# Two-layer decoder on one core: weight buffers cut into 1 MiB slots, the second round of an expert set moved, one loop over the set pairs

## The chip, the cores and the metric

The kernel runs on one core of a Trainium2 chip. The metric is the device time of one execution in microseconds; lower is better. One stretch of the clock of TensorE matters below: the profile shows which share of full speed (2.4 GHz) was granted, 1.0 or 0.5 (1.2 GHz).

## The reference, cut to what matters

Two layers over 256 tokens of width 1024, all float32. Each layer is attention and then a mixture of 32 experts.

```python
x = x + concat[DiffAttn(h), StickBreaking(h)] @ w_out[l]        # h = rms_norm(x) @ w_in[l], 3072 columns
h2 = rms_norm(x)
# routing: the best group of 4, then the best 2 of its 8 experts
hg = einsum('sd,edf->sef', h2, w_gate)      # w_gate, w_up: (32, 1024, 256)
hu = einsum('sd,edf->sef', h2, w_up)
act = silu(hg) * hu * combine[..., None]    # combine is zero but for 2 experts of a token
x = x + einsum('sef,efd->sd', act, w_down)  # w_down: (32, 256, 1024)
```

All 32 experts' weights are read in each layer: 3 MiB an expert, 96 MiB a layer, beside 16 MiB of `w_in` and `w_out`.

## The kernel before, in words

Every engine has its own program, and semaphores tie them together. SyncE (`SP`) issues the weight DMAs in one order written by hand; TensorE (`PE`) multiplies; VectorE (`DVE`) and ScalarE (`ACT`) copy PSUM banks out and do the pointwise work.

Attention of a layer: `proj_tile` multiplies the normed tokens with six blocks of `w_in` (2 MiB each, 512 columns), the heads' scores and sums follow, and `out_proj` uses two blocks of `w_out`.

Experts of a layer: they are done in 8 sets of 4 (`LANES`). Of each expert up to 32 tokens (`SLOTS`) are taken in a round, so that 4 experts fill the 128 rows. One set is, in TensorE's order in `expert_set`: `gate_up` (64 matmul records, two for each float32 matmul, from gate and up weights of 4 experts), `gather` of the tokens of the following set (32 records), `transpose_weights` for it, `transpose_act`, `down` (32 records), `scatter` back to the tokens (8 records). If an expert of the set has more than 32 tokens, a second round is done by the branches on `most > SLOTS`: before, `early` (its gather, its transpose of the weights, its `gate_up`) stands between the first round's `transpose_act` and its `down`, and `late` (its `down` and `scatter`) at the set's end. Rounds three and up are in `further_rounds`; when there is no second round TensorE branches over `late` and `whole`, and increments seven or eight semaphores (L333) in their place.

TensorE's sets stand in a loop over pairs of sets (a set with even number and one with odd number use other slots of the weight buffer). Before, it is two loops: three passes over the pair's code, and a second copy of that code for the last pair, which reads the last `w_down` elsewhere. VectorE and ScalarE have one loop each.

Weight buffers before: `wbuf` has slots of 2 MiB and `dnbuf` holds the four `w_down` of a set. SyncE's `load_rest` waits for `slot_used` (the set before has done its `gate_up` in all its rounds), issues one gate, then the next set's lane 0, then waits for `dn_used`, issues the four `w_down` and the rest of the next set's gate and up.

VectorE in a set: `select` for the following set (and for the second round), `activate`, `act_copy` (which lets `down` start), `gather_copy`, `y_copy`, `into_x`.

## Time and profile before

| what | value |
|---|---|
| time, median of 3 runs | 855.61 us (848.56, 855.61, 856.1) |
| span of the profiled execution | 850.2 us, first to last instruction |
| granted TensorE clock, mean of the span | 0.940 |
| busy: PE, DVE, ACT | 687.0, 310.9, 123.8 us |
| read from HBM | 238.54 MB, 282 GB/s over the span |
| experts of layer 0 / of layer 1 | about 175.7 to 424 us / 594.5 to 845 us |

The profiled execution's time from start to end of the device's work isn't listed apart from its span; the median of the runs is 5.4 us above the span. A line number such as L1159 is the line of the kernel before; `PEldq` is TensorE's instruction sequencer; "issue" is time of an engine for which the profile shows no awaited work. Profiles number the microseconds from the first instruction.

### The profile page before, as it was taken

The page shows a single profiled execution, that of the slowest core. Times are in us where ns is not written, and L with a number is a line of the kernel's source. Part 1 is how long each engine was busy: PE and PEld are TensorE (multiplying, and loading weights), DVE is VectorE, ACT ScalarE, POOL GpSimd, SP SyncE. Part 2 cuts the span into 40 slices and gives each one's busy share as a digit, 9 for nine tenths or more (in the row PEclk, how much of TensorE's full clock was granted, in tenths as well). Part 3 has the DMA queues.
Part 4 walks back from the last instruction along what each step waited for, and adds up shares of the span by engine and source line. Part 5 has one row for each costly group of instructions (what it writes and reads, how often), then busy time and mean ns, then how long its engine had stood idle before and what let it go on. Part 6 is the DMA issues. An engine that isn't in the chain of part 4 may idle for free.

```text
span 850.2 us, 10581 instructions
## 1 busy us (share of the span) xinstructions
PE 687.0 (81%) x3752; PEld 341.8 (40%) x3753; DVE 310.9 (37%) x692; ACT 123.8 (15%) x302; POOL 9.0 (1%) x19
## 2 busy tenths in 40 slices
PE   7998999887487487787799989997874874777885
PEld 4445464553133133252344445647331331332423
DVE  0437622543223223333325363425332331333333
ACT  3115421200000000000031343211000000000100
POOL 0000000010000000000020000000000000000000
PEclk9998999999889799899999999998987997998999
DMA  8894046759999999957297220492599999999441
GB/s 288 275 391 161 1 180 269 292 116 383 417 419 402 419 398 420 420 228 310 90 356 285 100 99 24 182 422 115 190 423 417 373 422 418 387 422 420 183 167 52
DMA packets 49815, 240.93 MB, mean 283 GB/s; under 512 B 7424, under 2 KB 7712, under 8 KB 25152
## 3 DMA queue, kind: packets, MB, share of 16 engines
q1 hardware_dynamic: 49120, 238.61, 70.4%
q0 software_dynamic: 608, 0.99, 1.0%
q8 instruction: 74, 1.21, 0.6%
q14 instruction: 13, 0.11, 0.0%
HBM read 238.54 MB, written 1.05 MB: 282 GB/s over the span
## 4 chain that ended last, share of the span: by engine, by line
PE 66%; issue 17%; PEldq 5%; DVE 4%; ACT 2%; PEld 2%; DVEq 1%; DMA 1%; ACTq 1%; SPq 0%
PE bank L1014 18%; PE bank L1159 17%; PE bank L1140 9%; PE bank L1185 7%; PE bank L1112 6%; PEldq L1178 4%; PE bank L1071 1%; ACT qkT L533 1%; PE bank L1058 1%; PEld bank L1176 1%; PE bank L1176 1%; DMA wbuf<-in_w_in 1%; PE bank L1091 1%; PE bank L1034 1%; PEldq L1323 1%
## 5 line engine op out<-in xcount | busy, mean ns | idle before, releaser
L1159 PE MATMUL bank<-wbuf,qkT 128*32 128x512 f32 x1024 | 137.7, 686 | 80.8 <-issue 79.6
L1014 PE MATMUL bank<-wbuf,hTbuf 128*128 128x512 f32 x384 | 170.1, 600 | 2.5 <-DMA wbuf<-in_w_in 2.0
L1159 PEld LDWEIGHTS bank<-wbuf,qkT 128*32 128x32 f32 x1024 | 39.1, 124 | 176.9 <-issue 175.3
L1014 PEld LDWEIGHTS bank<-wbuf,hTbuf 128*128 128x128 f32 x384 | 72.5, 192 | 90.8 <-issue 88.5
L1140 PE MATMUL bank<-qkT,xn 128*128 128x128 f32 x576 | 70.1, 281 | 20.2 <-issue 20.2
L1140 PEld LDWEIGHTS bank<-qkT,xn 128*128 128x128 f32 x576 | 67.0, 195 | 34.7 <-issue 34.6
L787 DVE TENSOR_TENSOR x_sb<-x_sb,bank 128x512 f32<-128x512 f32 x72 | 46.2, 684 | 77.2 <-PE bank L1185 77.2
L1176 PE MATMUL bank<-dnbuf,qkT 128*32 128x512 f32 x512 | 61.6, 597 | 11.4 <-DVE qkT L776 7.7
L764 DVE TENSOR_SCALAR qkT<-qkT 128x256 f32<-128x256 f32 x18 | 5.3, 294 | 156.4 <-ACT qkT L529 156.4
L1112 PE MATMUL bank<-wbuf,hTbuf 128*128 128x512 f32 x128 | 56.0, 593 | 0.0
L529 ACT ACTIVATE qkT<-bank 128x256 f32<-128x256 f32 x18 | 6.9, 384 | 287.5 <-PEq L1162 287.5
L1185 PE MATMUL bank<-qkT,hTbuf 128*128 128x512 f32 x80 | 36.7, 601 | 8.4 <-ACT qkT L533 8.4
L1112 PEld LDWEIGHTS bank<-wbuf,hTbuf 128*128 128x128 f32 x128 | 23.9, 190 | 27.7 <-issue 27.7
L1176 PEld LDWEIGHTS bank<-dnbuf,qkT 128*32 128x32 f32 x512 | 15.1, 109 | 49.5 <-issue 49.3
L1185 PE MATMUL bank<-qkT 128*128 128x512 f32 x64 | 29.3, 600 | 5.4 <-ACT qkT L533 5.4
L766 DVE RECIPROCAL qkT<-qkT 128x256 f32<-128x256 f32 x18 | 31.5, 1752 | 1.4
L474 ACT ACTIVATE wbuf<-bank,rstd 128x512 f32<-128x512 f32 x24 | 16.4, 684 | 78.8 <-PE bank L1014 78.5
L1185 PEld LDWEIGHTS bank<-qkT,hTbuf 128*128 128x128 f32 x80 | 14.4, 189 | 31.5 <-issue 31.5
L525 ACT COPY qkT<-bank 128x512 f32<-128x512 f32 x18 | 10.6, 586 | 90.0 <-PE bank L1140 90.0
L533 ACT COPY qkT<-bank 128x512 f32<-128x512 f32 x18 | 10.6, 586 | 87.8 <-PEq L1178 87.8
L1185 PEld LDWEIGHTS bank<-qkT 128*128 128x128 f32 x64 | 11.5, 190 | 22.1 <-issue 22.1
L780 DVE COPY qkT<-bank 128x512 f32<-128x512 f32 x18 | 12.4, 690 | 18.7 <-PEq L1178 18.7
(187 smaller groups left out, 580.9 us busy)
## 6 DMA issues: line engine op xcount, KB each, us to landing
wbuf<-in_w_gate SPq DMA_DIRECT2D x64, 1024.0 KB, 12.5
wbuf<-in_w_up SPq DMA_DIRECT2D x64, 1024.0 KB, 16.8
dnbuf<-in_w_down SPq DMA_DIRECT2D x56, 1024.0 KB, 10.7
wbuf<-in_w_in SPq DMA_DIRECT2D x10, 2048.0 KB, 18.4
wbuf<-in_w_out SPq DMA_DIRECT2D x4, 2048.0 KB, 18.0
wbuf<-in_w_down SPq DMA_DIRECT2D x8, 1024.0 KB, 12.2
wbuf<-in_w_in SPq DMA_DIRECT2D x4, 1024.0 KB, 8.5
x_sb<-in_x SPq DMA_DIRECT2D x2, 512.0 KB, 4.1
```

Source lines behind the costliest of these rows:

```text
L474: nc.scalar.activation(dst, ps[PROJ_BANK[i][t]][:, :], ACT.Copy, scale=rstd[:, t:t + 1]).then_inc(proj_out, 1)
L533: nc.scalar.copy(y[:, HALF:], ps[5][:, :]).then_inc(s["y_a"], 1)
L766: V.reciprocal(rg, rg)
L780: V.tensor_copy(y[:, 0:HALF], ps[4][:, :]).then_inc(s["y_d"], 1)
L787: last = V.tensor_tensor(x_sb[:, t, c], x_sb[:, t, c], ps[SC_BANK[t][h]][:, :], ALU.add)
L1014: last = MM(ps[PROJ_BANK[i][t]][:, :], hT[:, k, t * P:(t + 1) * P], w[:, k, :], start=(k == 0), stop=(k == KC - 1))
L1112: last = MM(ps[OP_BANK[t][h]][:, :], hT[:, k, t * P:(t + 1) * P], w[:, k, :], start=(k == 0), stop=(k == KC - 1))
L1140: last = MM(ps[k // 4][:, (k % 4) * P:(k % 4 + 1) * P], xn[:, t, k * P:(k + 1) * P], sel[:, t, :], start=(t == 0), stop=(t == TT - 1))
L1159: MM(ps[2][j * SLOTS:(j + 1) * SLOTS, :].rearrange("p (a f) -> p a f", a=2), src[:, k, j * SLOTS:(j + 1) * SLOTS], halves[:, gate:up + 1:u ...
L1176: MM(ps[4 + h][j * SLOTS:(j + 1) * SLOTS, :], actT[:, c, j * SLOTS:(j + 1) * SLOTS], at[j][:, c * D + h * HALF:c * D + (h + 1) * HALF], st ...
L1178: pe.drain().then_inc(s[f"dn{h}_ps"], 1)
L1185: last = MM(ps[SC_BANK[t][h]][:, :], weights[:, t, :], y[:, h * HALF:(h + 1) * HALF], start=True, stop=True)
```

## The change

- One buffer of 19 slots of 1 MiB holds all weights and the attention's scratch. Which slot holds what is a table with a period of two sets (`GATE_SLOT`, `UP_SLOT`, `DOWN_SLOT`, `BLOCK_SLOT`). The total stays 19 MiB.
- SyncE's program is written out set by set, without its loop. It waits for the products themselves (`proj_ps`, `qkT_ps`, `o_ps`, `oproj_ps`) in the attention, and for `gu_used` and `dn_used`, one count for each set, among the experts. After the last set it loads three blocks of the next layer's `w_in` at once, and the rest behind the last `gate_up` and `down`.
- TensorE has one loop over four pairs instead of three passes and a copy.
- The second round: its gather and weight transposes stand at the set's start, its `gate_up` right behind that of the first round (in PSUM bank 3), its `transpose_act` and `down` after the first round's `scatter` has been added in.
- VectorE does `gather_copy` before `act_copy`, no longer behind it. Reading `most` moves from behind `gate_up` to the set's start.

```diff
-        wbuf = sb("wbuf", [P, (SLOTS_W + 1) * SLOT + SLOT // 2])
-        dnbuf = sb("dnbuf", [P, LANES, FC * D])
+        wbuf = sb("wbuf", [P, SLOTS_W * SLOT])
...
+            def load_further_sets(l):
+                for g in range(1, SETS):
+                    if g > 1:
+                        for j in range(LANES - 1):
+                            load_up(l, g, j)
+                    sp_.wait_ge(gu_used, l * SETS + g)
+                    load_up(l, g, LANES - 1)
+                    if g + 1 < SETS:
+                        for j in range(LANES):
+                            load_gate(l, g + 1, j)
+                    sp_.wait_ge(dn_used, l * SETS + g)
                     for j in range(LANES):
+                        load_down(l, g, j)
+            def load_next_layer(l):
+                for i in range(3):
+                    load_block(l, i)
+                sp_.wait_ge(gu_used, l * SETS)
+                load_block(l, 3)
+                load_block(l, 4)
+                sp_.wait_ge(dn_used, l * SETS)
+                load_block(l, 5)
+                load_half(l, IN_BLOCKS, 0)
...
             def expert_set(l, g, parity):
                 most = dve.value_load(cnt[0:1, bass.ds(g, 1)], min_val=0, max_val=SEQ)
...
+                with dve.If(most > SLOTS):
+                    select(more, g, 1, sel_more, selw_more)
+                    gather_copy(more, dve.snap(g * MORE + (l * SETS * MORE + 1)), hgT_more, selwT_more, more_half)
                 dve.wait_ge(first["selwT_ps"], g + (l * GATHERS + 1))
                 select(first, g + 1, None, sel, selw)
-                with dve.If(most > SLOTS):
-                    select(more, g, 1, sel_more, selw_more)
                 n = dve.snap(g + l * SETS + 1)
-                activate(first, n)
-                act_copy(first, n)
-                gather_copy(first, dve.snap(g + l * GATHERS + 2), hgT, selwT2[1 - parity], 6)
+                activate(first, n, FIRST_GU)
+                gather_copy(first, dve.snap(g + l * GATHERS + 2), hgT, selwT2[1 - parity], first_half)
+                act_copy(first, n, first_half)
+                with dve.If(most > SLOTS):
+                    activate(more, dve.snap(g * MORE + (l * SETS * MORE + 1)), MORE_GU)
                 y_copy(first, n)
...
-            def expert_set(l, g, parity, last):
-                for j in range(LANES):
-                    pe.wait_ge(gu_in[parity][j], g * 16 + (l * SETS + 2 - parity) * 16)
-                gate_up(first, g + (l * GATHERS + 1), hgT, l, parity)
+            def expert_set(l, pair, parity):
+                g = pe.snap(pair * 2 + parity)
                 most = pe.value_load(cnt[0:1, bass.ds(g, 1)], min_val=0, max_val=SEQ)
                 n = pe.snap(g + l * SETS + 1)
...
+                with pe.If(most > SLOTS):
+                    m = pe.snap(g * MORE + (l * SETS * MORE + 1))
+                    pe.wait_ge(first["hg_d"], g + (l * GATHERS + 1))
+                    pe.wait_ge(first["hg_a"], g + (l * GATHERS + 1))
+                    pe.wait_ge(x_moe, n)
                     pe.wait_ge(x_more, m)
                     gather(more, m, sel_more)
+                    transpose_weights(more, m, more_half, selw_more)
+                arrived = pe.snap(pair * 16 + (l * SETS // 2 + 1) * 16)
+                for j in range(LANES):
+                    pe.wait_ge(gate_in[parity][j], arrived)
+                    pe.wait_ge(up_in[parity][j], arrived)
+                gate_up(first, pe.snap(g + (l * GATHERS + 1)), FIRST_GU, hgT, parity)
+                with pe.If(most > SLOTS):
+                    m = pe.snap(g * MORE + (l * SETS * MORE + 1))
+                    gate_up(more, m, MORE_GU, hgT_more, parity)
                     pe.wait_ge(more["selwT_out"], m)
+                with pe.If(most <= 2 * SLOTS):
+                    pe.sem_inc(gu_used, 1)
+                following = pe.snap(g + (l * GATHERS + 2))
+                gather(first, following)
...
+                def late(m):
+                    pe.wait_ge(x_moe, g + (l * SETS + 2))
+                    transpose_act(more, m, more_half)
+                    down(more, m)
...
-                with pe.Fori(0, SETS // 2 - 1) as pair:
-                    expert_set(l, pe.snap(pair * 2), 0, False)
-                    expert_set(l, pe.snap(pair * 2 + 1), 1, False)
-                with pe.Fori(SETS // 2 - 1, SETS // 2) as pair:
-                    expert_set(l, pe.snap(pair * 2), 0, False)
-                    expert_set(l, pe.snap(pair * 2 + 1), 1, True)
+                with pe.Fori(0, SETS // 2) as pair:
+                    for parity in range(2):
+                        expert_set(l, pair, parity)
```

## Rows read from the trace of the kernel before

**Rows 1.** The page: busy time of the engines, the chain's shares by engine

```profile
PE 687.0 (81%) x3752; PEld 341.8 (40%) x3753; DVE 310.9 (37%) x692; ACT 123.8 (15%) x302; POOL 9.0 (1%) x19
...
PE 66%; issue 17%; PEldq 5%; DVE 4%; ACT 2%; PEld 2%; DVEq 1%; DMA 1%; ACTq 1%; SPq 0%
```

**Rows 2.** Chain of waits in order of time: start us, us, what

```profile
223.40 10.84 issue
234.23 9.80 PE bank L1159 x64
...
259.13 2.11 issue
261.24 2.77 PE bank L1159 x21
264.01 1.02 issue
265.03 5.34 PE bank L1159 x43
270.37 1.26 issue
...
346.71 4.56 issue
351.27 9.31 PE bank L1159 x64
...
644.61 11.05 issue
...
679.37 3.61 issue
682.98 8.77 PE bank L1159 x64
691.75 1.28 issue
693.03 3.83 PE bank L1140 x32
...
768.57 4.99 issue
```

**Rows 3.** The gate weights that set 4 needs last: their issue, then landing

```profile
L360 SPq DMA_DIRECT2D wbuf<-in_w_gate x1: 333/333/333, 271.5 to 271.5; - x1
...
DMA to landing us min/median/max: 13.0/13.0/13.0
```

**Rows 4.** Waits of SyncE's queue: us in total, times, longest us

```profile
SPq L360 <- PEq L1195: 203.3, 12, 27.8
```

**Rows 5.** Chain of waits between 637 and 732 us, one loop-back step by step

```profile
705.53 3.34 issue
708.87 0.07 PEldq L331
...
710.47 6.05 PEldq L1323
```

**Rows 6.** Branches and reads of TensorE's sequencer: ns min/median/max, first and last start

```profile
L1323 PEldq COMPARE_BRANCH  x6: 76/6009/6189, 227.6 to 772.9; - x6
...
L1245 PEldq COMPARE_BRANCH  x16: 68/226/362, 193.8 to 839.0; - x16
...
L1190 PEldq EVENT_SEMAPHORE  x22: 51/51/51, 173.6 to 820.9; - x22
```

**Rows 7.** DMA queue of the instructions: packets, MB, share

```profile
q8 instruction: 74, 1.21, 0.6%
```

**Rows 8.** TensorE's timeline through set 6 (layer 0), with second round

```profile
367.09 3.84 PE L1140 MATMUL bank<-hTbuf,xn 128*128 128x128 f32 x32 [1.11 <-DVE qkT L758]
370.76 0.38 PE L1147 MATMUL bank<-cst,hTbuf 128*128 128x128 f32 x2
371.71 7.07 PE L1159 MATMUL bank<-wbuf,hTbuf 128*32 128x512 f32 x64 [0.56 <-DVE hTbuf L758]
...
387.82 3.96 PE L1176 MATMUL bank<-dnbuf,qkT 128*32 128x512 f32 x32
392.59 3.67 PE L1185 MATMUL bank<-qkT,hTbuf 128*128 128x512 f32 x8 [0.81 <-ACT qkT L533]
```

**Rows 9.** VectorE's timeline between 365 and 368 us

```profile
366.01 0.42 DVE L776 COPY qkT<-bank 128x256 f32<-128x256 f32 x1 [1.61 <-PE bank L1167]
366.35 0.68 DVE L758 COPY qkT<-bank 128x512 f32<-128x512 f32 x1
366.95 0.41 DVE L760 COPY hTbuf<-bank 128x256 f32<-128x256 f32 x1
```

**Rows 10.** Busy time by stretches of 10 us (PE, PEld, DVE, ACT, POOL; clock, DMA share, GB/s)

```profile
350.00:360.00 10.00, 8.73 (x64) 2.55 (x64) 3.16 (x17) 0.00 (x0) 0.00 (x0) 0.71 1.01 419
...
370.00:380.00 10.00, 8.79 (x83) 3.21 (x85) 1.66 (x4) 0.97 (x2) 0.00 (x0) 1.00 0.11 43
```

More of the change, by code:

```diff
@@ L302, in decoder @@
         GATHERS = SETS + 1
-        def second_round_early(eng, n_set, most, early):
-            with eng.If(most > SLOTS):
-                early(eng.snap(n_set * MORE + 1))
         def further_rounds(eng, n_set, most, late, whole, owed):
@@ L533, in y_copy, with whole, expert_set @@
                 nc.scalar.copy(y[:, HALF:], ps[5][:, :]).then_inc(s["y_a"], 1)
-            def early(n):
-                gather_copy(more, n, hgT_more)
-                gate(more, n)
-            def late(n):
-                y_copy(more, n)
-            def whole(n, r):
-                early(n)
-                late(n)
+            def whole(m, r):
+                gather_copy(more, m, hgT_more)
+                gate(more, m, MORE_GU)
+                y_copy(more, m)
+            def expert_set(l, g):
+                most = act.value_load(cnt[0:1, bass.ds(g, 1)], min_val=0, max_val=SEQ)
+                n = act.snap(g + l * SETS + 1)
+                with act.If(most > SLOTS):
+                    gather_copy(more, act.snap(g * MORE + (l * SETS * MORE + 1)), hgT_more)
+                gate(first, n, FIRST_GU)
+                with act.If(most > SLOTS):
+                    act.wait_ge(first["act_out"], n)
+                    gate(more, act.snap(g * MORE + (l * SETS * MORE + 1)), MORE_GU)
+                gather_copy(first, act.snap(g + l * GATHERS + 2), hgT)
+                y_copy(first, n)
+                further_rounds(act, g + l * SETS, most, lambda m: y_copy(more, m), whole, ACT_MORE)
             for l in range(DEPTH):
@@ L609, in _ @@
                 with act.Fori(0, SETS) as g:
-                    most = act.value_load(cnt[0:1, bass.ds(g, 1)], min_val=0, max_val=SEQ)
-                    gate(first, act.snap(g + l * SETS + 1))
-                    gather_copy(first, act.snap(g + l * GATHERS + 2), hgT)
-                    second_round_early(act, g + l * SETS, most, early)
-                    y_copy(first, act.snap(g + l * SETS + 1))
-                    further_rounds(act, g + l * SETS, most, late, whole, ACT_MORE)
+                    expert_set(l, g)
         @block.vector
@@ L754, in select, with gather_copy @@
                 select_weights(s, [wgg[:, t, :] for t in range(TT)], sel, selw)
[L756 removed]
+            def gather_copy(s, n, dst, dst_w, half):
                 dve.wait_ge(s["gathered"], n)
@@ L1208, in early @@
                     gather(more, m, sel_more)
-                    transpose_weights(more, m, 7, selw_more)
-                    gate_up(more, m, hgT_more, l, parity)
+                    transpose_weights(more, m, more_half, selw_more)
+                    gate_up(more, m, MORE_GU, hgT_more, parity)
+                    transpose_act(more, m, more_half)
+                    down(more, m)
                     pe.wait_ge(more["selwT_out"], m)
-                    with pe.If(most <= 2 * SLOTS):
-                        pe.sem_inc(slot_used, LANES)
@@ L1215, in late @@
-                def late(m):
-                    pe.wait_ge(more["actT_out"], m)
-                    pe.wait_ge(x_moe0, n)
-                    down(more, l, last)
-                    with pe.If(most <= 2 * SLOTS):
-                        pe.sem_inc(dn_used, 1)
-                    pe.wait_ge(x_moe, g + (l * SETS + 2))
-                    scatter(more, m, selwT_more)
-                def whole(m, r):
+                    scatter(more, m, selwT_more)
+                with pe.If(most > SLOTS):
[3 more added lines that the diff above has]
+                    pe.wait_ge(x_moe, n)
@@ L1225, in whole @@
                     pe.wait_ge(x_more, m)
                     gather(more, m, sel_more)
-                    transpose_weights(more, m, 7, selw_more)
-                    gate_up(more, m, hgT_more, l, parity)
-                    transpose_act(more, m)
-                    pe.wait_ge(more["actT_out"], m)
-                    down(more, l, last)
-                    pe.wait_ge(more["selwT_out"], m)
-                    scatter(more, m, selwT_more)
-                second_round_early(pe, g + l * SETS, most, early)
@@ L1243, in expert_set @@
+                pe.wait_ge(x_moe, n)
+                pe.wait_ge(x_more, g * MORE + (l * SETS * MORE + 1))
+                pe.wait_ge(first["selwT_out"], g + (l * GATHERS + 1))
+                transpose_weights(first, following, first_half)
+                transpose_act(first, n, first_half)
+                for j in range(LANES):
+                    pe.wait_ge(dn_in[j], g * 16 + (l * SETS + 1) * 16)
+                down(first, n)
                 with pe.If(most <= SLOTS):
                     pe.sem_inc(dn_used, 1)
-                with pe.If(most > SLOTS):
-                    transpose_act(more, pe.snap(g * MORE + (l * SETS * MORE + 1)))
```

293 lines of the change are left out of this document (132 added, 161 removed).

## The prediction

> **What bounds the kernel now.** I read the page first, then the chain of waits in order of time. In the experts' stretch the DMA engines look full (419 GB/s in a typical 10 us [rows 10]), so the first guess is that weights pace the sets. The chain says otherwise: 66% of the span is TensorE at work, 17% "issue", and 1% DMA [rows 1]. Each set's chain runs `gate_up`, `gather`, `down`, `scatter` and then an "issue" piece before the next `gate_up`. The length of that piece alternates: 10.84 us before set 2, 2.11 before set 3, 11.05 before set 2 of layer 1, 3.61 before set 3 [rows 2]. A late weight would show as a landing just before `gate_up`. Set 4's last one is issued at 271.5 and lands 13.0 later, at 284.5 [rows 3]; that set's `gate_up` starts only at 295.8. SyncE meanwhile waits 203.3 us in total for TensorE to give slots back [rows 4]. So the weights are ahead and TensorE's own program is the limit, narrowly: a pair of sets takes 61.6 us (`gate_up` of set 2 to that of set 4), and its 24 MiB (25.2 MB) take 60 us at 419 GB/s.
>
> What fills the 11 us before even sets? The step-by-step view of one of them shows two waits of the sequencer: 3.34 us after the `scatter`, for the branch over the second round's code, and 6.05 us in the branch that closes the loop, L1323 [rows 5]. L1323 runs six times and its median is 6.0 us, its minimum 0.076 [rows 6]. The short ones are the two exits of the first loop, where TensorE falls through into the copy of the code for the last pair; there "issue" is only 4.56 and 4.99 us [rows 2]. A jump to code that isn't at hand costs 6 us, going straight on does not.
>
> The Trainium skill has a rule for this ("Runtime: NRT & Kernel Launch", Instruction fetch mechanics): instructions come in blocks of 16 KiB or 256 instructions, the next block is fetched while one executes, and a taken branch to a target outside a window of two blocks waits for a fetch. The trace agrees on the size (the instruction queue moved 1.21 MB in 74 packets, 16 KB each [rows 7]) and on the loop's branch.
>
> **The change part by part.** Sums are against the profiled execution, span 850.2 us; the runs' median of 855.6 stands 5.4 above it, and I carry that over.
>
> (a) *One loop of four passes for three passes and a copy.* Each layer gets a third loop-back in place of the straight entry: the mean of 10.84 and 11.05 is 10.9, that of 4.56 and 4.99 is 4.8, so +6.1 a layer, +12 us. Nothing hides it: the chain is on TensorE there. The lower bound is 0 (if the entry into set 6 were waiting for something else), the upper 2 x 6.2 [rows 6].
>
> (b) *The head of a set.* Reading `most` moves from behind `gate_up` to ahead of it; both places are on the chain, so that is nothing. New are: one more passed-over block ahead of `gate_up` and one behind it (median of a short branch 0.226 us [rows 6], 0.3 with the gap behind it, each), four more waits that come two to an instruction (2 x 0.05 and their gaps, 0.2) and two register operations (0.2): 1.0 us a set. In the first set of a layer VectorE's copies cover it, in odd sets the wait of (d); six sets are left, +6 us. Bounds 0 and 16.
>
> (c) *`act_copy` behind `gather_copy`.* `down` waits for `act_copy`. Now the copies of the gathered tokens and of the weights go first: they take from 366.35 to 367.36, 1.0 us [rows 9]. TensorE's `transpose_weights` and `transpose_act` hide 0.4 of it, since `gather_copy` can start when `gather` ends. +0.6 us a set, 16 sets, +10 us. What is later for it on VectorE is only `y_copy`. Bounds 0 and 16 x 1.0.
>
> (d) *Odd sets.* In set 3 `gate_up` stops after 21 matmul records for 1.02 us, and nothing of the other engines releases it; it goes on at 265.03, 5.9 us after the `scatter`'s end at 259.13 [rows 2]. I read this as the next piece of code arriving about 6 us after the branch over the second round, 42 instructions into `gate_up`. With the change a stretch of 68 instructions (the second round's `gather` and weight transposes: 64 and 4) stands ahead of `gate_up` and is passed over, so TensorE needs that piece before its first matmul, and the first third of `gate_up` no longer covers the wait. `gate_up` starts about 5.5 us after the `scatter`, and after such a pause it runs at the lower clock for a while: 9.31 us after a pause of 4.56 [rows 2], where the granted clock of the stretch was 0.71 [rows 10], against 7.07 in one without a pause [rows 8]. From `scatter` to `gather` that makes 5.5 + 9.3 + 0.9 = 15.7 us; in set 3 of layer 0 it is 12.5 (259.13 to 271.63), in layer 1 13.7 (679.37 to 693.03). +3.2 and +2.0 for each of three odd sets, +16; set 7 of either layer has other neighbours before, and I put 1 and 2 on it: 18.6, of which I take two thirds, because the branch ahead resolves up to 1 us earlier in the new order: +12 us. No row shows the new layout. Bounds: 0, if the piece is there in time; 16 sets x 3 = 48, if each of the new forward branches waits as that one.
>
> By that rule of the Trainium skill, a forward branch over less than one block of 256 instructions finds its target in the window, so (d) would be 0 and the sum 28; the pause inside `gate_up`, in straight code, shows that the next block isn't always there, and I go by the row.
>
> (e) *The second round,* set 6 in both layers. Before, 49.6 us from 346.71 to the end of `late`'s `scatter` at 396.26. Its matmuls are the same. Gained: the gather no longer waits 1.11 us for the copies and `gate_up` no longer 0.56 [rows 8], as both have other work ahead of them. Lost: `late` before starts `down` at 387.82, at the very end of the first `scatter`, since its activations were ready; now `transpose_act` waits for the last addition into `x`, 0.7 + 0.1, then 0.4 for itself and 0.5 for the copy, 1.8 in all. Net about nothing, +0.1 a layer. Bounds -2 and +4 a layer.
>
> (f) *Slots, order of loads, `gu_used` given back earlier.* Before, in set 6 the release waits for the second `gate_up`, which stands behind two gathers, and the DMA engines fall to 43 GB/s from 370 to 380 [rows 10]. The new order releases some 10 us earlier and this hole goes. It is worth nothing while TensorE is the limit: set 7's `gate_up` starts right behind set 6's `scatter`. The same for the three blocks of `w_in` loaded early: DMA is 1% of the chain [rows 1]. If weights did pace the stage, it would be worth what the rival below says. SyncE's written-out program is issued far ahead.
>
> Sum: 12 + 6 + 10 + 12 + 0 = +40 us. Span 890, time 855.6 + 40 = 896.
>
> **The rivals.** *Nearby code is always at hand.* (d) is 0, and so is half of (b): 12 + 3 + 10 = +25, 881 us. The rule of the Trainium skill cited above would give this. For it: even sets show no pause inside `gate_up` [rows 2]. Against: set 3's pause.
>
> *Each new forward branch waits.* Two stretches of code are passed over in each set without second round, 14 a layer. If half of them wait 2 us, +28 more: 925 us. For it, the 6 us of L1323; against, the 0.226 us of short branches [rows 6].
>
> *Weights pace the sets.* Then the earlier release decides: the hole of about 8.6 us in each layer (10 us at 43 instead of 419 GB/s is 9.0) goes, and with smaller dips some 4 us a layer: 855.6 - 25 = 831 us. It decides from the point where TensorE's pair of sets is shorter than 60 us; it is 61.6 now and gets longer by (a) to (d). Against it also rows 3. This is the one on the faster side.
>
> *The loop-back is hidden or the code stays at hand.* If a loop-back costs no more than going on, and (d) is 0, (b) and (c) are left, partly covered by the wait for weights that would then come last: 855.6 + 5 = 861 us.
>
> **How the numbers follow.** Forecast 0.55; nearby code at hand 0.24; each branch waits 0.08; weights pace 0.06; loop-back hidden 0.07. The forecast's own range is 885 to 912. To leave out no more than 2 in 10 the range takes in the first rival and the upper bounds of (b) and (c): 872 to 917. One per cent, 8.6 us, is what a measurement of this kernel can tell from no change (its three runs lie 7.5 apart). Slower by over 1% (above 864): 0.55 + 0.24 + 0.08 and a little of the last, 0.88; within 1%: 0.06; faster: 0.06.
>
> **What would show it.** (a) The loop's branch near 6 us in six of its eight executions, where four of six were before, and 11 us of issue before set 6 in place of 4.6. (b) The reading of `most` ahead of `gate_up`, and `gather` within 0.9 us of it instead of 1.3. (c) `down` 1.6 us behind `gather` instead of 1.0. (d) no split of `gate_up` in odd sets, but 5 us or more of issue ahead of it. (f) no hole in the DMA rate during set 6, and more waiting of SyncE in total. I am wrong if a `gate_up` starts within 0.5 us of its weights' landing in most sets, or if "issue" in the chain falls.

## The result and the profile after

| what | before | after |
|---|---|---|
| time, median of 4 runs each, in us | 855.06 (848.56 to 856.1) | 898.82 (894.23 to 905.57) |
| span of the profiled execution | 850.2 | 897.9 |
| granted TensorE clock, mean | 0.940 | 0.911 |
| experts of layer 0 (first `gate_up` to last `scatter`) | 246.5 | 275.8 |
| experts of layer 1 | 248.7 | 266.4 |

The ratio is 1.0539, with a 95% interval of 1.0467 to 1.0611: slower, by 43.8 us against a forecast of 40.

The page of after, beside [rows 1]. TensorE's matmuls are the same 3752 records; they take 12 us more. "issue" has grown from 17% of a shorter span to 19% of a longer one, 145 us to 171, and DMA is still 1%.

```profile
PE 698.9 (78%) x3752; PEld 350.5 (39%) x3753; DVE 310.6 (35%) x692; ACT 124.0 (14%) x302; POOL 9.0 (1%) x19
...
PE 64%; issue 19%; DVE 6%; PEldq 5%; ACT 2%; DVEq 2%; PEld 1%; DMA 1%; ACTq 0%; SPq 0%
```

The chain of waits of after in order of time (start, us, what), which answers to [rows 2]:

```profile
195.91 9.13 issue
...
228.61 12.75 issue
...
265.32 8.02 issue
...
333.52 5.86 issue
...
675.07 11.99 issue
...
710.04 3.55 issue
...
737.16 12.02 issue
...
773.52 6.18 issue
```

Read the "issue" pieces by their place. Ahead of even sets (228.61, 675.07, 737.16) they are 12 to 12.8 us, where they were 10.8 to 11.1. Ahead of odd sets of layer 0 (195.91, 265.32, 333.52) they are 9.13, 8.02 and 5.86, where before's chain has 1.99, 2.11 and 2.51. In layer 1, whose code is a second copy of the same instructions, they are 4.85, 3.55 and 6.18 against 4.19, 3.61 and 4.22. No odd set's `gate_up` of after stops inside: the row of 21 matmuls and the 1.02 us of [rows 2] have no successor there. In before only the three odd sets of layer 0 stop; those of layer 1 run through their 64 records [rows 2].

Branches of TensorE's sequencer and the wait of SyncE, as [rows 6] and [rows 4] (ns min/median/max; us in total, times, longest):

```profile
L1302 PEldq COMPARE_BRANCH  x8: 76/5976/6455, 233.4 to 892.7; - x8
...
L1197 PEldq COMPARE_BRANCH  x16: 80/332/3594, 172.9 to 866.3; - x16
...
L1210 PEldq COMPARE_BRANCH  x18: 84/229/436, 181.4 to 876.2; - x18
```

```profile
SPq L335 <- PEq L1215: 313.4, 14, 33.8
```

L1302 is the loop's branch; it runs eight times and costs 6.0 us as before. L1197 and L1210 are the branches over the second round's code ahead of `gate_up` and behind it. The row of SyncE and that of [rows 4] are each one of three: SyncE's waits for TensorE's counts among the experts are 361 us before (203.3, 93.3 and 64.2) and 443 after (313.4, 85.5 and 44.0), so the weights are further ahead than they were. TensorE's timeline through set 6 of layer 0, beside [rows 8]:

```profile
375.59 5.49 PE L1124 MATMUL bank<-hTbuf,xn 128*128 128x128 f32 x32 [11.67 <-issue]
381.23 7.07 PE L1143 MATMUL bank<-wbuf,qkT 128*32 128x512 f32 x64
388.81 7.08 PE L1143 MATMUL bank<-wbuf,hTbuf 128*32 128x512 f32 x64 [0.51 <-issue]
402.03 3.95 PE L1160 MATMUL bank<-wbuf,qkT 128*32 128x512 f32 x32 [1.10 <-DVE qkT L768]
...
412.82 5.50 PE L1160 MATMUL bank<-wbuf,qkT 128*32 128x512 f32 x32 [0.52 <-DVE qkT L768]
```

The 11.67 us ahead of the first gather is the third loop-back of the layer; before, 4.56 us stood there [rows 2].

Busy time by stretches of 10 us, after (columns as in [rows 10]):

```profile
380.00:390.00 10.00, 9.49 (x88) 3.53 (x90) 3.42 (x12) 0.97 (x2) 0.00 (x0) 1.00 0.20 83
390.00:400.00 10.00, 9.22 (x86) 5.24 (x79) 1.99 (x3) 0.38 (x1) 0.00 (x0) 1.00 0.21 79
400.00:410.00 10.00, 7.99 (x49) 3.05 (x47) 6.10 (x10) 1.17 (x2) 0.00 (x0) 1.00 0.07 28
410.00:420.00 10.00, 7.16 (x38) 1.73 (x37) 2.47 (x5) 0.59 (x1) 0.00 (x0) 0.83 0.05 7
```

The hole in the DMA rate of set 6 has not gone. It is wider: 83, 79, then 28 and 7 GB/s, where before had one such stretch in set 6.

**Where the 47.7 us of span went.** From the starts and ends of `gate_up`, `gather` and `scatter` in both timelines:

| stretch | predicted | measured |
|---|---|---|
| (a) pause between `scatter` of set 5 and the first matmul of set 6, two layers | +12 | +14.4 (7.1 and 7.3) |
| (b) `scatter` to `gather` of even sets 2 and 4, both layers (+1.0, +1.0, -0.2, +1.4), and `gate_up` to `gather` of set 0 (-1.2) | +6 | +2.0 |
| (c) start of `gather` to end of `scatter`, 14 sets, 13.5 us before and 13.8 after | +10 | +4.7 |
| (d) `scatter` to `gather` of sets 1, 3, 5 (+15.6 and +2.7) and 7 (+0.8 and +2.9) | +12 | +22.0 |
| (e) the rest of set 6 | 0 | +3.9 |
| outside the experts (layer 1's attention +2.2, ahead of set 0 -1.5) | 0 | +0.7 |
| sum | +40 | +47.7 |

The predicted 6 us of (b) are for six sets. Their share for set 6 is measured in row (a), since a set's head and the pause ahead of it are one stretch there.

### The profile page after: what moved, and what is told of

The parts are those of the page before. It is cut to its first block, busy times and chain, and to the rows that moved or that the text cites. A ratio compares the mean times of both kernels' runs of the same rounds, so it can differ in the third digit from the quotient of the medians.

```text
span 897.9 us, 10392 instructions
## 1 busy us (share of the span) xinstructions
PE 698.9 (78%) x3752; PEld 350.5 (39%) x3753; DVE 310.6 (35%) x692; ACT 124.0 (14%) x302; POOL 9.0 (1%) x19
## 4 chain that ended last, share of the span: by engine, by line
PE 64%; issue 19%; DVE 6%; PEldq 5%; ACT 2%; DVEq 2%; PEld 1%; DMA 1%; ACTq 0%; SPq 0%
PE bank L999 17%; PE bank L1143 17%; PE bank L1124 9%; PE bank L1169 7%; PE bank L1096 6%; PEldq L1162 4%; ACT qkT L523 1%; PE bank L1056 1%; PEld bank L1160 1%; PE bank L1043 1%; DVE qkT L750 1%; PE bank L1076 1%; DMA wbuf<-in_w_in 1%; PE bank L1019 1%; PE bank L1069 1%
## 5 line engine op out<-in xcount | busy, mean ns | idle before, releaser
L1143 PE MATMUL bank<-wbuf,qkT 128*32 128x512 f32 x1024 | 137.9, 699 | 95.3 <-issue 94.2
L1143 PEld LDWEIGHTS bank<-wbuf,qkT 128*32 128x32 f32 x1024 | 38.6, 126 | 190.8 <-issue 189.2
L1160 PE MATMUL bank<-wbuf,qkT 128*32 128x512 f32 x576 | 72.5, 622 | 20.5 <-DVE qkT L768 18.6
L1160 PEld LDWEIGHTS bank<-wbuf,qkT 128*32 128x32 f32 x576 | 16.9, 111 | 63.9 <-issue 62.4
L1124 PE MATMUL bank<-hTbuf,xn 128*128 128x128 f32 x64 | 10.7, 344 | 24.0 <-issue 24.0
L1169 PEld LDWEIGHTS bank<-qkT,hTbuf 128*128 128x128 f32 x80 | 14.4, 189 | 31.3 <-issue 31.3
L772 DVE COPY qkT<-bank 128x512 f32<-128x512 f32 x18 | 12.4, 690 | 37.2 <-PEq L1162 37.2
L750 DVE COPY qkT<-bank 128x512 f32<-128x512 f32 x18 | 12.5, 692 | 35.6 <-PE bank L1124 35.6
L523 ACT COPY qkT<-bank 128x512 f32<-128x512 f32 x18 | 10.6, 586 | 102.9 <-PEq L1162 102.9
## 6 DMA issues: line engine op xcount, KB each, us to landing
wbuf<-in_w_gate SPq DMA_DIRECT2D x64, 1024.0 KB, 10.8
```

The lines of the kernel that those rows point to most:

```text
L523: nc.scalar.copy(y[:, HALF:], ps[5][:, :]).then_inc(s["y_a"], 1)
L750: V.tensor_copy(dst[:, 0:4, :], ps[0][:, :].rearrange("p (k s) -> p k s", k=4)).then_inc(s["hg_d"], 1)
L1124: last = MM(ps[k // 4][:, (k % 4) * P:(k % 4 + 1) * P], xn[:, t, k * P:(k + 1) * P], sel[:, t, :], start=(t == 0), stop=(t == TT - 1))
L1143: MM(ps[bank][j * SLOTS:(j + 1) * SLOTS, :].rearrange("p (a f) -> p a f", a=2), src[:, k, j * SLOTS:(j + 1) * SLOTS], halves[:, gate:up + ...
L1160: MM(ps[4 + h][j * SLOTS:(j + 1) * SLOTS, :], actT[:, c, j * SLOTS:(j + 1) * SLOTS], at[j][:, c * D + h * HALF:c * D + (h + 1) * HALF], st ...
L1169: last = MM(ps[SC_BANK[t][h]][:, :], weights[:, t, :], y[:, h * HALF:(h + 1) * HALF], start=True, stop=True)
```

## The experiments

Theory: the program of TensorE sets the end, and what is lost is waiting for its code. Rivals: the order of VectorE's copies; the weights; the layout or order of sets itself. Ratios are to the kernel before on the same chip. All diffs are against after, unless it says before. Times taken on one chip compare best, since the kernel before itself had medians of 849.0 to 855.1 on the four chips. Each kernel has one trace, and its own executions lie up to 14 us apart (11 in after), so a single pause that differs by a few microseconds between two traces need not come from the edit.

**split**: three passes of the loop and a copy for the fourth, as before.

```diff
-                with pe.Fori(0, SETS // 2) as pair:
-                    for parity in range(2):
-                        expert_set(l, pair, parity)
+                for start, stop in ((0, SETS // 2 - 1), (SETS // 2 - 1, SETS // 2)):
+                    with pe.Fori(start, stop) as pair:
+                        for parity in range(2):
+                            expert_set(l, pair, parity)
```

> The changed kernel with TensorE's loop of four passes undone: three passes and a second copy of the code for the last pair, as in the kernel before; all else as changed. Theory A (a jump back costs a fetch of code, step (a) of the prediction): one loop-back of about 12.5 us of pause per layer becomes a straight entry of about 5 to 7 us, so 11 to 14 us less than the changed kernel, near 886 us; the loop's branch near 6 us in four executions, not six. Theory B (the loss is the order on TensorE and VectorE) or theory C (the new order of loads): no change, near 899.

886.34 us, ratio 1.0477 (1.0373 to 1.0581). The chain around set 6 of layer 0, and the loop's branch:

```profile
354.54 3.69 PE bank L1169 x8
...
363.81 6.69 PE bank L1124 x32
```

```profile
L1303 PEldq COMPARE_BRANCH  x8: 76/3021/6522, 229.8 to 879.0; - x8
```

The pause from 358.23 to 363.81 is 5.6 us, where after has 11.7; in layer 1 it is 5.4 for 12.3. Together 13.0, and the profiled spans differ by 13.5. The median is 12.5 below that of after, and 11.0 below that of act_first on the same chip, a kernel as slow as after. The median of the branch lies between a long and a short one, since only four of eight are long now. The intervals of the two ratios overlap, so the size rests on the chain more than on the times. Before has 4.56 and 4.99 at this place: the 1.4 us that are left are the longer head of the set, step (b).

**straight**: the four pairs written out.

```diff
-                with pe.Fori(0, SETS // 2) as pair:
-                    for parity in range(2):
-                        expert_set(l, pair, parity)
+                for start in range(SETS // 2):
+                    with pe.Fori(start, start + 1) as pair:
+                        for parity in range(2):
+                            expert_set(l, pair, parity)
```

> The changed kernel with TensorE's code for the pairs written out four times, so that there is no jump back at all. Theory A: three loop-backs per layer become straight entries, 6 x 6 to 7 us = 36 to 42 us less than the changed kernel, near 860 us, as long as weights don't become the limit (24 MiB a pair take 60 us; a pair would take about 60 to 61). The pauses of 3 to 6 us before odd sets stay. Theory B or C: near 899.

875.05 us, 1.0324 (1.0224 to 1.0425): a gain of 24 instead of 36 to 42. In the trace the six pauses that had a loop-back are 34 us shorter in sum, but the six ahead of odd sets are 7.8 longer than in after (45.4 for 37.6), where I had expected them to stay. No loop-back is left, and 5.3 to 10.8 us still stand ahead of sets 1 to 6. The waits of TensorE on "issue" ahead of `gate_up` (us in total, times, longest):

```profile
PE bank L1143 <- issue: 81.6, 14, 10.8
```

Each set without a second round branches over `late` and over all the code for rounds three and up. In this trace no pause behind that branch is shorter than 5.5 us ahead of sets 1 to 5, without any loop-back; set 7 has 3.3 and 3.6.

**act_first**: VectorE's `act_copy` ahead of `gather_copy` again.

```diff
-                gather_copy(first, dve.snap(g + l * GATHERS + 2), hgT, selwT2[1 - parity], first_half)
                 act_copy(first, n, first_half)
+                gather_copy(first, dve.snap(g + l * GATHERS + 2), hgT, selwT2[1 - parity], first_half)
```

> The changed kernel with VectorE's act_copy put back ahead of gather_copy. Step (c) of the prediction: 0.5 to 0.6 us in each of 16 sets, so 8 to 10 us less than the changed kernel, near 890 us, and gather to down 5.9 us instead of 6.4. Theory A alone or theory C: no change.

897.36 us, 1.0565 (1.0464 to 1.0667): 1.5 less than after and not 8 to 10, though four executions each, spread over 11 us, can hardly tell 1.5 from 8. Two sets of its chain:

```profile
196.53 9.88 issue
206.40 9.88 PE bank L1143 x64
...
217.21 3.83 PE bank L1124 x32
...
226.85 3.67 PE bank L1169 x8
230.53 11.75 issue
```

From the start of `gather` (217.21) to the end of `scatter` (230.52) it is 13.3 us, 0.5 less than after in each set, so the copies' order did cost that. But the pauses before odd sets are 9.88, 6.29 and 6.47 in layer 0 and 6.86, 8.25 and 5.94 in layer 1: 43.7 in total against 37.6 of after. In this pair of traces the wait for code took back most of what the shorter sets gave. TensorE's program is the same in both kernels, instruction for instruction, yet the pause ahead of set 3 of layer 1 is 8.25 us here and 3.55 in after. Such pauses are not a property of the code alone.

**before_straight**: the kernel before with its four pairs written out.

```diff
-                with pe.Fori(0, SETS // 2 - 1) as pair:
-                    expert_set(l, pe.snap(pair * 2), 0, False)
-                    expert_set(l, pe.snap(pair * 2 + 1), 1, False)
-                with pe.Fori(SETS // 2 - 1, SETS // 2) as pair:
-                    expert_set(l, pe.snap(pair * 2), 0, False)
-                    expert_set(l, pe.snap(pair * 2 + 1), 1, True)
+                for start in range(SETS // 2):
+                    with pe.Fori(start, start + 1) as pair:
+                        expert_set(l, pe.snap(pair * 2), 0, False)
+                        expert_set(l, pe.snap(pair * 2 + 1), 1, start == SETS // 2 - 1)
```

> The kernel before with TensorE's code for the pairs written out four times. Theory A: two loop-backs per layer go, 4 x 6 = 24 us, but a pair of sets then takes TensorE 55.5 us and the weights 60, so weights become the limit of the middle pairs and only a part comes: 8 to 14 us less than before, near 843 us, with DMA landings just before gate_up. If weights were the limit already, or the loop-back not the cause: no change, 855.

840.08 us, 0.9888 (0.9808 to 0.9967), as expected, and here weights begin to end last: DMA is 7% of the chain, with three sets that wait for `w_gate`. One of them, landing and start of `gate_up`:

```profile
326.96 19.51 DMA wbuf<-in_w_gate
...
346.83 9.16 PE bank L1159 x64
```

Written out, the two kernels are still 35 us apart.

**gather_behind**: the second round's gather and weight transposes moved behind the first `gate_up`, so that nothing is passed over ahead of it.

```diff
+                arrived = pe.snap(pair * 16 + (l * SETS // 2 + 1) * 16)
+                for j in range(LANES):
...
+                gate_up(first, pe.snap(g + (l * GATHERS + 1)), FIRST_GU, hgT, parity)
                 with pe.If(most > SLOTS):
...
                     transpose_weights(more, m, more_half, selw_more)
-                arrived = pe.snap(pair * 16 + (l * SETS // 2 + 1) * 16)
-                for j in range(LANES):
...
-                gate_up(first, pe.snap(g + (l * GATHERS + 1)), FIRST_GU, hgT, parity)
-                with pe.If(most > SLOTS):
-                    m = pe.snap(g * MORE + (l * SETS * MORE + 1))
                     gate_up(more, m, MORE_GU, hgT_more, parity)
```

> The changed kernel with the second round's gather and weight transposes moved from the set's head to right behind the first round's gate_up, so that only one stretch of code is passed over in a set without second round, and none ahead of gate_up. Theory A, step (d): the pauses before the six odd sets without second round (9.1, 8.0, 5.9, 4.9, 3.6, 6.2 us in the changed kernel) fall to 2 to 5 us, partly given back as a stop inside gate_up; 10 to 16 us less than the changed kernel, near 886. Rival: those pauses come from elsewhere in the code's layout and stay; then within 4 us of 899 (the second round itself gets about 1 us longer in two sets).

900.41 us, 1.0555 (1.0452 to 1.0659): no gain, where 886 was expected. The profiled execution is the longest of its four, 906.8. Pauses before odd sets are 5.19, 5.36, 5.10 and 5.72, 5.42, 5.35, far more even than after's, and none near the 2 us of before. In layer 1 `gate_up` now stops inside and takes over 11 us. From `scatter` to `gather` the six odd sets take 99.7 us together, where after has 98.5 and before 80.2. This speaks against (d) as I read it: taking the passed-over stretch from ahead of `gate_up` doesn't bring before's short pauses back.

**quarter**: from the third set on only a quarter of each expert's weights is loaded. The arithmetic goes on with what the slots hold; this kernel leaves out three quarters of those sets' weights.

```diff
-                sp_.dma_start(slot(at), w_gate_e[l * EXPERTS + g * LANES + j]).then_inc(gate_in[g % 2][j], 16)
+                n = SLOT if g < 2 else SLOT // 4
+                sp_.dma_start(slot(at)[:, 0:n], w_gate_e[l * EXPERTS + g * LANES + j][:, 0:n]).then_inc(gate_in[g % 2][j], 16)
```

(the same for `w_up_e` and `w_down_e`)

> The changed kernel, but from the third set of each layer on only the first quarter of each expert's gate, up and down weights is loaded (the rest is left from an earlier set): 54 MiB less per layer. If weights paced the sets anywhere, well over 10 us would go. Theory A with a fixed cost of fetching code: within 4 us of 899, the loop's branch still near 6 us. Theory A with fetches that stand in line behind weight traffic: the loop's branch falls to 3 to 4 us and the pauses with it, 15 to 30 us less, near 875.

865.03 us, 1.0181 (1.0085 to 1.0277): 34 us less than after, with DMA at 1% of the chain in both. Its loop's branch and its chain:

```profile
L1305 PEldq COMPARE_BRANCH  x8: 76/4371/4913, 232.4 to 856.3; - x8
```

```profile
229.39 8.67 issue
...
262.50 3.25 issue
265.75 7.07 PE bank L1146 x64
```

The long branches take 4.4 us instead of 6.0, the pauses before even sets 8.5 to 10 and before odd ones 3.25. No weight was waited for in after, yet fewer weights make TensorE's code arrive sooner. The nearest reading is that the fetches of the program stand in line with the kernel's own transfers. Sets 1, whose weights are still loaded whole, pause longer than the odd sets behind them: 5.19 and 4.02 us against 3.25 to 3.34.

**straight_two**: written out as in straight, and in place of `further_rounds` only the second round (this input has no third).

```diff
-                further_rounds(pe, g + l * SETS, most, late, whole, PE_MORE)
+                two_rounds(pe, g + l * SETS, most, late, PE_MORE)
```

> The changed kernel with the pairs written out four times and without TensorE's code for rounds three and up (never executed on this input, some 300 of the 400 instructions that TensorE passes over at a set's end). Theory A: the pause before each gate_up falls to 2 to 4 us; a pair then takes TensorE about 53 us, so weights pace the stage at 60 us a pair: near 830 us. If TensorE's jumps are not the cause: as the written-out kernel, 875.

**before_straight_two**: the same two edits in before.

> The kernel before with the pairs written out four times and without TensorE's code for rounds three and up. TensorE is then no longer the limit in the middle sets of either order, and the difference between this and the same edit of the changed kernel is what slots and order of loads are worth. Step (f): the hole in the DMA rate in set 6 stays here; 5 to 15 us more than the other if weights pace, near 838 (840 for the written-out kernel before). If TensorE's own order still decides, this one stays the faster: near 825.

843.5 us, 0.9926 (0.9877 to 0.9974), and 830.49 us, 0.9753 (0.9674 to 0.9832). The first was expected near 830, the second near 838 if weights paced and near 825 if TensorE's order still decided. Leaving out code that is never executed gives 4 points of ratio over straight and 1.4 over before_straight. The chain's shares by engine, straight_two and then before_straight_two:

```profile
PE 57%; DMA 17%; issue 10%; DVE 5%; PEldq 4%; ACT 2%; DVEq 2%; PEld 1%; SPq 1%; ACTq 1%
```

```profile
PE 52%; DMA 20%; issue 13%; DVE 4%; PEld 3%; PEldq 3%; ACT 2%; DVEq 1%; ACTq 1%; SPq 0%
```

A middle set in the chain of each, in the same order:

```profile
248.74 21.81 DMA wbuf<-in_w_down
```

```profile
233.47 20.52 DMA wbuf<-in_w_gate
```

Now the weights end last in most middle sets: with the code out of the way TensorE overtakes them. In after's order it is `down` that waits, in before's the next `gate_up`. Here the 19 slots of 1 MiB and their earlier release had their chance, and the old kernel is 13 us faster (9.0 between the profiled spans). From the end of set 2's `scatter` to that of set 5 the three middle sets take 89.9 us in after's order and 91.7 in before's in layer 0, 89.1 and 93.3 in layer 1. So the new order is ahead where weights pace, by 1.8 and 4.1 us; but it also comes to these sets 2.9 and 2.8 us later, so part of that is waiting that it no longer has to do. It loses in the others: sets 6 and 7 together take 77.9 and 78.2 us against 74.2 and 73.3, and sets 1 and 2 of layer 0 take 26.3 and 26.9 against 23.4 and 25.0. The head of one such set, in each kernel:

```profile
198.37 3.04 issue
201.41 8.76 PE bank L1155 x64
```

```profile
199.51 1.90 issue
201.41 7.07 PE bank L1171 x64
```

The stretches of that `gate_up` by the granted clock (PE, PEld, DVE, ACT, POOL; clock, DMA share, GB/s), again straight_two and then before_straight_two:

```profile
201.40:204.40 3.00, 2.99 (x16) 0.94 (x20) 1.50 (x8) 0.00 (x0) 0.00 (x0) 0.50 1.03 423
204.40:207.40 3.00, 3.00 (x29) 0.92 (x25) 0.00 (x0) 0.00 (x0) 0.00 (x0) 0.93 1.03 423
```

```profile
201.40:204.40 3.00, 2.99 (x28) 1.10 (x32) 1.03 (x7) 0.00 (x0) 0.00 (x0) 1.00 1.00 421
```

After 3.04 us without a matmul the clock was at its lower level, 1.2 GHz, for the first 3 us; after 1.90 us it had stayed at 2.4. So in this pair of sets the head of (b), 1.1 us longer, was followed by a `gate_up` that took 1.7 more.

**before_block**: before, with the reading of `most` ahead of `gate_up` and 68 instructions behind it that are always passed over.

```diff
-                gate_up(first, g + (l * GATHERS + 1), hgT, l, parity)
                 most = pe.value_load(cnt[0:1, bass.ds(g, 1)], min_val=0, max_val=SEQ)
+                with pe.If(most > 2 * SLOTS):
+                    keep_clock(17)
+                gate_up(first, g + (l * GATHERS + 1), hgT, l, parity)
```

> The kernel before, with most read ahead of gate_up and a stretch of 68 instructions ahead of gate_up that is passed over in every set: steps (b) and (d) of the prediction alone. By the prediction: 6 + 12 = 18 us more, 873. After the earlier runs I expect that a stretch ahead of gate_up only moves where the waiting shows: the number of code blocks that a pair runs through decides, here 7.7 instead of 7.4, and 5 to 18 us come, in pauses ahead of odd sets. If forward branches are free: 3 us or less.

863.71 us, 1.0159 (1.0093 to 1.0224), 13.9 over before on the same chip. The profiled execution was its quickest, 853.7. Pauses in layer 0:

```profile
195.86 5.87 issue
...
225.69 12.09 issue
...
261.14 5.18 issue
...
289.13 3.48 issue
```

Odd sets now pause 5.87 and 5.18 where before had 1.99 and 2.11, and no `gate_up` stops inside. From `scatter` to `gather` the six odd sets take 90.1 us together for 80.2. The edit does that; the run doesn't part the stretch from the earlier reading of `most`, nor from the code of each set being longer. The 3.48 is ahead of set 4, a loop-back whose code was at hand. The loop's branch and the instruction queue of this execution say the same, three long branches instead of four and 71 packets where before has 74 [rows 7]:

```profile
L1325 PEldq COMPARE_BRANCH  x6: 76/3138/6197, 229.9 to 773.4; - x6
```

```profile
q8 instruction: 71, 1.16, 0.5%
```

Why the code was at hand, the profile doesn't show. Part of the gain was lost again, since set 6 then waited for weights until 345.42 and another 7.62 us behind that. Without the quick loop-back I estimate this execution at 860 us: 8.6 more ahead of set 4 (12.1 for 3.48), 2.4 less ahead of set 6 (5.6 as in layer 1 for 7.99). The other five are 862 to 867.

**shifted**: after, and 128 instructions ahead of each layer's loop that are never executed.

```diff
+                with pe.If(pe.value_load(cnt[0:1, 0:1], min_val=0, max_val=SEQ) > 2 * SLOTS):
+                    keep_clock(32)
                 with pe.Fori(0, SETS // 2) as pair:
```

> The changed kernel with 128 instructions more of never executed code ahead of the loop of each layer, half a block of code: nothing else differs. Theory A: where the pauses fall depends on where the code's blocks begin; the sum over a layer moves by up to 10 us one way or the other, and the pauses before odd sets become other ones. If the pauses come from anything but the code's place in memory, they stay as in the changed kernel, and the time within 3 us of 899.

905.78 us, 1.0666 (1.0597 to 1.0734). That is 7 us over after, on another chip and with overlapping intervals, so a shift of the time is likely and not shown. The work is after's; only what lies behind sits elsewhere. Its chain in layer 0:

```profile
196.53 5.50 issue
...
225.72 14.22 issue
...
263.47 5.71 issue
```

9.13, 12.75, 8.02 of after have become 5.50, 14.22, 5.71: the odd sets won 3.6 and 2.3, the even one lost 1.5. In layer 1 it was the other way for the odd ones (5.85, 6.28, 8.98). The experts' stretch of layer 0 is 3 us shorter, that of layer 1 7 longer. None of these pauses changed by more than the 4.7 us between after and act_first, whose TensorE programs are the same and in the same place. So shifted doesn't show that the place of the code decides.

**straight_two_act**: straight_two with the copies in the order of act_first.

> The changed kernel written out, without the code for rounds three and up, and with act_copy ahead of gather_copy. In that kernel (843) no fetch of code stands on the path. Step (c) by itself: 0.5 us in each of 10 sets that don't wait for weights, 5 us less, near 838. If (c) is free: 843.

842.81 us, 0.9912 (0.9873 to 0.9952): 0.7 less than straight_two, not 5, with ten executions of each. Start of `gather` to start of `down` is 4.85 us instead of 5.35, but the middle sets wait for weights instead (DMA is 20% of the chain for 17%).

**two_paths**: before's buffers and order, and both forms of the loop. VectorE adds the layer's greatest count to `cnt`; up to two rounds TensorE takes the pairs written out without rounds three and up, else the two loops as before.

```diff
+                top = pe.value_load(cnt[0:1, SETS:SETS + 1], min_val=0, max_val=SEQ)
+                with pe.If(top <= 2 * SLOTS):
+                    for start in range(SETS // 2):
+                        with pe.Fori(start, start + 1) as pair:
+                            expert_set(l, pe.snap(pair * 2), 0, False, True)
+                            expert_set(l, pe.snap(pair * 2 + 1), 1, start == SETS // 2 - 1, True)
+                with pe.Else():
...
```

> A complete version on the basis of the kernel before: VectorE also takes the greatest count of the layer; where it is at most 64, TensorE runs through the pairs written out, without the code for rounds three and up; otherwise through the loops of before. Theory A: 830 of the written-out kernel without that code plus one long jump per layer of about 6 us, partly beside VectorE's last additions, near 838 us, ahead of before (850) and of the written-out kernel before (840). If the saving depended on the shorter program and not on the way through it: near 850.

838.05 us, 0.9852 (0.9783 to 0.992): faster than both kernels for this input, which has at most two rounds. The code for more rounds is there, but no run took that path, so neither its time nor its result is shown. It pays for the jump over the other path and for adding one reduction; before_straight_two, without them, has 0.9753.

**Packets of the instruction queue.** One number of every kernel's page, as [rows 7] shows it for before, goes with these times:

| order | kernel: packets, median us |
|---|---|
| after's | after: 78, 898.82; split: 74, 886.34; straight: 67, 875.05; straight_two: 48, 843.5 |
| before's | before: 74, 855.06; before_straight: 67, 840.08; two_paths: 52, 838.05; before_straight_two: 48, 830.49 |

Within each order fewer packets go with less time; split has two loop-backs fewer than after and four packets fewer. The number alone isn't the price: quarter moves 78 packets as after does, in 865 us, and at equal numbers before's order is the faster.

## Why the prediction was right, and where it wasn't

The forecast of 896 was met by 898.8, the span's sum of 40 by 47.7. That the total came within 3 us is in part luck: (b) and (c) were 9.3 too high together, the other rows 17 too low. Its cause, TensorE's walk through its own program, is shown: the pauses are there with all weights landed, go with the loop's form (split) and with the length of code passed over (straight_two against straight).

**(a)** was right in place and nearly in size: 14.4 in the chain, of which 13.0 go when split undoes it, for 12. The other 1.4 are the head of set 6, which belongs to (b).

**(b)** was too high: 6 for 2.0, or 3.4 with the head of set 6. The pauses ahead of even sets 2 and 4 are 0.9 to 1.9 us longer, more than the 1.0 of my sum, but the `gate_up` behind three of the four is 0.2 to 0.6 shorter, and `gather` follows `gate_up` 0.2 to 0.7 sooner in sets 0 to 5, since the reading of `most` no longer stands between. I put both places on the chain and called their difference nothing, then added new branches on top; the sum should have had the gain per set as a term against the new branches.

**(c)** was right as a mechanism and too high, 10 for 4.7. `down` waits 1.10 us for the copy where it waited 0.61, so 0.5 a set for my 0.6, 6.9 us in 14 sets; but five of these sets took 13.6 to 13.8 us before already, three of them with a stop inside `down` (0.28 to 0.46 us), and after has 13.8 in every one. What I had not seen is that it may not be worth undoing: act_first wins 0.5 us in each of these stretches, 7 in all, and 1.5 in time; straight_two_act, where weights wait instead, wins 0.7. A term on the path isn't a gain when taken away if the next thing on the path arrives by its own clock.

**(d)** is the term that was mis-sized, 22.0 for 12, and its reading holds only in part. That the pause inside `gate_up` turns into a longer one ahead of it was right in layer 0: no `gate_up` of an odd set stops in after, and before_block, which does (b) and (d) together, costs 13.9; in its trace the six odd sets take 9.9 more. In layer 1 before has no such stop, and there sets 1, 3 and 5 gave 2.7 us of the 18.3. But the single value, 5.5 us before each odd set, is wrong: 9.13, 8.02 and 5.86 in one layer, 4.85, 3.55 and 6.18 in the other, from the same instructions. Nor is the stretch the whole: gather_behind takes it away and keeps 5.1 to 5.7. What my step had left out is that one piece of code at one place has no single wait: the loop of layer 0 has 9.13, 8.02 and 5.86 in three passes, and act_first, with TensorE's program unchanged, has 8.25 where after has 3.55. Whether the place of the code counts as well stays open. I took one set's 42 instructions as the law for all; the two layers of before would have warned me, since the layer-0 and layer-1 rows of the same set differ already (2.11 and 3.61 in [rows 2]). The cut to two thirds, from 18.6 to 12, had no row behind it; the uncut sum was nearer to the 22.0.

**(e)** was near: +3.9 in two layers for 0, within its bounds of -4 and +8. Two of the waits that I named are there (1.10 us for the copy, 0.52 in the second `down`); where the rest comes from, no run takes apart.

**(f)** was right that it is worth nothing, and wrong in what the profile would show: the hole in the DMA rate was to go, and grew. SyncE waits longer in total, as said. The earlier release was to be worth something if weights paced the stage, some 12 us a layer by the rival's sum. In straight_two and before_straight_two weights do pace the middle sets, and after's arrangement takes 1.8 and 4.1 us less in them, at most; as a whole it is 13 us slower.

**The rivals.** *Nearby code is always at hand* (881) is refuted by the pauses before odd sets. The rule of the Trainium skill behind it ("Runtime: NRT & Kernel Launch", Instruction fetch mechanics), that a taken branch waits only for a target outside the window of two blocks, agrees with the loop's branch here. I had used it for the short new stretches only, and of their branches L1210 never takes over 0.44 us, L1197 up to 3.6. At a set's end TensorE also branches over `late` and `whole`, some 400 instructions by my count and so more than one block, and there the rule allows a wait without any loop; straight_two, which drops some 300 of them, agrees with 3.0 to 3.6 us ahead of sets 1 to 5. How long such a wait is, it doesn't say. Its sentence that kernels "prefer full unrolling where possible" agrees: writing the pairs out gained 24 us in after and 12 in before. *Each new forward branch waits* (925): L1197 has a median of 0.33 us and a maximum of 3.6, L1210 a maximum of 0.44, so most don't. *Weights pace the sets* (831): DMA stayed at 1% of the chain. *Loop-back hidden* (861): the branch kept its 6.0 us.

**Open.** Which block of the program is fetched when, and from which point a piece is late, no run shows. Why the same code waits 3.6 us in one execution and 8.2 in another is open, and so is whether the place of the code counts, since shifted moves the pauses no more than that. Why one loop-back of before_block was quick is open too, and the interplay in gather_behind of longer `gate_up` and even pauses was not taken apart. That fetches queue behind weight transfers is argued from quarter, the only run that changes that load; which part they share isn't shown.

## What to carry to other kernels

When the chain of waits has "issue" pieces of several microseconds on TensorE with its inputs long there, look at the branches: count the loop-backs and the code that is jumped over, and write out the path that the data take, with the rare path elsewhere (two_paths, 0.9852). Don't shorten work around such a pause before the pause itself is gone; here 7 us of shorter sets came out as 1.5, on four executions each. And judge a new buffer arrangement with the pause removed from both kernels: against each other they were 44 us apart, without it 13.

## What the runs showed of the hardware that I had not expected

- The time of a long branch depends on the DMA load: 6.0 us with full weights, 4.4 with a quarter of them from the third set on.
- With TensorE's program unchanged, the pause at one place was 3.55 us in one kernel's trace (after) and 8.25 in another's (act_first), and in three passes of one loop 9.13, 8.02 and 5.86.
- Code that is never executed costs time: without it the written-out kernels took 843.5 us for 875.05 and 830.49 for 840.08.
- 3.04 us without a matmul was followed by a granted clock of 0.50 and a `gate_up` of 8.76 us; 1.90 us by 1.00 and 7.07. The length of the pause alone doesn't settle it: in quarter 3.25 us was followed by 7.07.
